# A two-layer hybrid block and a second block on one core: the first mixer rewritten as one interleaved program

## The reference, cut to what matters

```
z = rms_norm(h, norm_mix[0]) @ hy_w_in[0]
# delta rule: r, k, v, and three low-rank inputs (288 columns), each mixed with the token before
zr = zr + (token_shift(zr) - zr) * mu
w_log = -softplus(-(w0 + tanh(wd) @ w_up)) - 0.5; decay = exp(-exp(w_log))
a = sigmoid(a0 + ad @ a_up); g = sigmoid(gd) @ g_up
state = state * w_t - (state @ kk_t) (kk_t * a_t) + v_t k_t      # for each token
o = state @ r_t;  y_a = (group_norm(o) + sum(r * k * r_k) * v) * g
# state space
x_t = lam_bar * x_(t-1) + b_bar @ u_t ;  y = gelu(real(c_mat @ x_t) + d_skip * u)
y_b = y * sigmoid(y @ w_glu + b_glu)
h = h + concatenate([y_a, y_b]) @ hy_w_out[0]
```

## Time and profile before

| | us |
|---|---|
| three runs, median (lowest, highest) | 3212.8 (3207.9, 3220.8) |
| the profiled execution, its own time | 3210.8 |
| its span, first to last instruction | 3209.0 |
| PE busy in the span | 2824.6 |
| DVE busy | 2236.2 |
| ACT busy | 1650.6 |

### The profile page before, as it was taken

The page is one execution under the profiler, slowest core; times in us unless marked ns, Lnnn a source line. Parts: engine busy times, 40 slices in busy tenths (PEclk is TensorE's granted clock), DMA queues, the critical chain, the costliest instruction groups (busy, mean ns, idle before and its releaser), DMA issues.

```text
span 3209.0 us, 44097 instructions
## 1 busy us (share of the span) xinstructions
PE 2824.6 (88%) x18534; PEld 2523.0 (79%) x18534; DVE 2236.2 (70%) x2274; ACT 1650.6 (51%) x1569; POOL 0.2 (0%) x4
## 2 busy tenths in 40 slices
PE   6467017999997989999999999999999988998999
PEld 5357007999987978888888888888888778998899
DVE  2421784455565548888888888888888856886687
ACT  2200004444465536777776777777777645345443
POOL 0000000000000000000000000000000000000000
PEclk9776558999999989999999999999999989999999
DMA  5100003445542429999999999999999843554453
GB/s 194 40 2 1 0 0 121 142 145 184 171 130 68 158 110 342 357 353 346 354 356 346 348 352 352 353 353 350 352 354 358 324 138 119 184 171 132 132 184 132
DMA packets 237717, 690.50 MB, mean 215 GB/s; under 512 B 10448, under 2 KB 169168, under 8 KB 178128
## 3 DMA queue, kind: packets, MB, share of 16 engines
q1 hardware_dynamic: 235440, 685.59, 59.2%
q10 hardware_dynamic: 2080, 2.10, 0.2%
HBM read 686.59 MB, written 1.05 MB: 214 GB/s over the span
## 4 chain that ended last, share of the span: by engine, by line
PE 67%; DVE 7%; DMA 4%; ACT 3%; DVEq 2%; issue 1%; PEld 0%; PEldq 0%; ACTq 0%; SPq 0%
PE ps L716 20%; PE ps L718 20%; PE ps L717 20%; DMA ring<-moe 3%; PE ps L1462 1%; DVE more_lo L3095 1%; PE ps L776 1%; DVE w_lo L3095 1%; PE ps L1510 1%; DVE w_lo L1632 1%; ACT arena L1581 1%; PE ps L909 1%; ACT w_hi L1616 1%; DVE mix L2355 1%; PE ps L946 0%
## 5 line engine op out<-in xcount | busy, mean ns | idle before, releaser
L1632 DVE TENSOR_TENSOR w_lo<-ring,w_hi 128x1024 fp32r<-128x1024 f32 x362 | 437.5, 1222 | 372.1 <-ACT w_hi L1616 368.1
L1616 ACT ACTIVATE w_hi<-ring 128x1024 fp32r<-128x1024 f32 x362 | 380.3, 1057 | 465.0 <-PE ps L718 440.6
L716 PE MATMUL ps<-x_hi,w_hi 128*128 128x256 f32 x1952 | 563.3, 289 | 33.6 <-DVE x_lo L2349 17.6
L718 PE MATMUL ps<-x_hi,w_lo 128*128 128x256 f32 x1952 | 558.1, 286 | 0.0
L717 PE MATMUL ps<-x_lo,w_hi 128*128 128x256 f32 x1952 | 558.1, 286 | 0.0
L3095 DVE TENSOR_TENSOR w_lo<-ring,w_hi 128x2048 fp32r<-128x2048 f32 x232 | 522.7, 2284 | 15.3 <-ACT w_hi L1584 13.7
L1584 ACT ACTIVATE w_hi<-ring 128x2048 fp32r<-128x2048 f32 x232 | 445.3, 1920 | 159.9 <-DMA ring<-moe 133.3
L716 PEld LDWEIGHTS ps<-x_hi,w_hi 128*128 128x128 f32 x1952 | 380.5, 195 | 39.8 <-issue 38.5
L717 PEld LDWEIGHTS ps<-x_lo,w_hi 128*128 128x128 f32 x1952 | 380.6, 195 | 0.3
L718 PEld LDWEIGHTS ps<-x_hi,w_lo 128*128 128x128 f32 x1952 | 380.3, 195 | 0.0
L1584 ACT ACTIVATE more_hi<-ring 128x2048 fp32r<-128x2048 f32 x115 | 220.7, 1919 | 122.9 <-DMA ring<-moe 111.2
(11 more groups left out here) (339 smaller groups left out, 5068.4 us busy)
## 6 DMA issues: line engine op xcount, KB each, us to landing
ring<-moe SPq DMA_DIRECT2D x347, 1024.0 KB, 6.3
more_raw<-moe SPq DMA_DIRECT2D x115, 1024.0 KB, 6.5
ring<-ffn_w_up SPq DMA_DIRECT2D x44, 1024.0 KB, 5.1
ring<-ffn_w_down SPq DMA_DIRECT2D x22, 1024.0 KB, 4.8
ring<-xa_w_kv SPq DMA_DIRECT2D x16, 1024.0 KB, 5.5
ring<-w_in SPq DMA_DIRECT2D x16, 1024.0 KB, 5.8
ring<-da_w_qkv SPq DMA_DIRECT2D x12, 1024.0 KB, 5.1
ring<-ff_w_gate SPq DMA_DIRECT2D x11, 1024.0 KB, 5.3
```

Of the source, the lines that this page charges most:

```text
L716: mm(o, lhs[0], rhs[0], start=start, stop=False)
L718: return mm(o, lhs[1], rhs[0], start=False, stop=stop)
L1616: nc.scalar.activation(w_hi[:, half_slot(at, half), :], ring[:, s_, half * 1024:half * 1024 + 1024], ACT.Copy).then_inc(hi_ready, 1)
L1632: nc.vector.tensor_tensor(w_lo[:, i, :], ring[:, s_, half * 1024:half * 1024 + 1024], w_hi[:, i, :], ALU.subtract).then_inc(lo_ready, 1)
```

## The change

The three parts of the mixer become one program for each engine (`pe_first_mixer`, `act_first_mixer`, `dve_first_mixer`), in which the work of the projections, the delta rule and the state-space half is interleaved by hand, and each hand-over has a semaphore of its own; the meetings of all engines are gone from the mixer.

- Load order: h, a narrow head of the small inputs and of the constants, the 288 columns, the two chunks for u, then the remaining small inputs and constants, then k, r, v.
- State-space half: eight half rounds of two state tiles; the table of waves is built in four parts of four state tiles, each when it is needed (`s5_table`). The real and imaginary products are no longer added on DVE: four products go to PE, which adds them (`s5_sum`). It has PSUM banks 4 to 7, the delta rule 0 to 3; its buffers lie over x_hi, x_lo, act_hi and act_lo.
- Delta rule: products and their copies take turns in its four banks. In the recurrence both halves alternate (`halves`), the product of kappa and v is made ahead for all chunks, and the state of each chunk has a buffer of its own, so the next state needs only beta·u; the output of a chunk is multiplied after its change of state. The first chunk has no product with the state, which is zero.
- Output projection: the rows of `hy_w_out` are exchanged, so the state-space half comes first; the first two of its four chunks are multiplied in halves around the group norm (`out_half`), inside the mixer. `pe_memory` starts with the sums of the memory norm and chunks 2 and 3.

The diff, cut to its core:

```diff
+            sp.dma_start(h[:, :, :], x_t.rearrange("(k p) n -> p k n", p=P)).then_inc(h_loaded, 16)
+            sp.dma_start(small_sb[:, 0:HEAD_W], small[:, 0:HEAD_W]).then_inc(head_loaded, 16)
+            sp.dma_start(const_sb[:, 0:CONST_HEAD_W], const[:, 0:CONST_HEAD_W]).then_inc(head_loaded, 16)
             hy = w["hy_w_in"][0]
-            stream_columns(sp, at, hy, 0, 3 * RW)
             stream(sp, at, hy[:, 3 * RW:3 * RW + 288], 288)
             stream_columns(sp, at, hy, 3 * RW + 288, 4 * RW + 288)
+            sp.dma_start(small_sb[:, HEAD_W:SMALL_W], small[:, HEAD_W:SMALL_W]).then_inc(small_loaded, 16)
+            sp.dma_start(const_sb[:, CONST_HEAD_W:CONST_W], const[:, CONST_HEAD_W:CONST_W]).then_inc(const_loaded, 16)
+            for c in (2, 3, 0, 1, 4, 5):
+                stream_columns(sp, at, hy, c * CH, (c + 1) * CH)
...
+        def halves():
+
             for t in range(RT):
-                cs, ts = slice(t * P, (t + 1) * P), slice(t * S, (t + 1) * S)
-                mm(banks(0, 2)[:, ts], sm("lora")[0:64, cs], zg[0:64, 0, :], start=True, stop=True)
-                mm(banks(2, 2)[:, ts], sm("lora")[64:128, cs], zg[64:128, 0, :], start=True, stop=True)
-            for t in range(RT):
-                cs, ts = slice(t * P, (t + 1) * P), slice(t * S, (t + 1) * S)
-                mm(banks(4, 2)[:, ts], sm("g_up")[:, cs], zg[:, 1, :], start=True, stop=False)
-                mm(banks(4, 2)[:, ts], sm("g_up2")[0:32, cs], zg[0:32, 2, :], start=False, stop=True)
-                mm(banks(6, 2)[:, ts], cst("heads"), work[:, ts], start=True, stop=True)
-            pe.drain().then_inc(met, 1)
-            pe.wait_ge(met, at.step("lora products, sums for kk"))
-            pe.drain().then_inc(met, 1)
-            pe.wait_ge(met, at.step("sigmoids"))
-            pe.drain().then_inc(met, 1)
-            pe.wait_ge(met, at.step("cumulated decays, root for kk"))
-            pe.drain().then_inc(met, 1)
-            pe.wait_ge(met, at.step("exponentials, kk"))
-            pe.drain().then_inc(met, 1)
-            pe.wait_ge(met, at.step("alpha, beta, kappa, rho"))
+                yield t, HALF[0]
+                yield (t + 2) % RT, HALF[1]
+
+        def by_tile(hs, pair, t, off=0):
+            return ps[hs, 2 * pair + t // 2, off + (t % 2) * C:off + (t % 2) * C + C]
...
+            def level(i):
+                pe.wait_ge(below_ready, i + 1)
+                if i:
+                    pe.wait_ge(level_added, i)
+                for j, hs in problems():
+                    last = mm(pbank(0)[hs, j, :], below[i % 2][hs, j, :], tri[hs, j, :], start=True, stop=True)
+                last.then_inc(across_done, 1)
+                pe.wait_ge(across_out, i + 1)
+                for j, hs in problems():
+                    mm(pbank(2)[hs, j, :], tri_t[hs, j, :], xbuf[hs, j, :], start=True, stop=True)
+                for j, hs in problems():
+                    last = mm(pbank(0)[hs, j, :], xbuf[hs, j, :], tri_t[hs, j, :], start=True, stop=True)
+                last.then_inc(level_done, 1)
+
+            def state_by_alpha(c):
+                pe.wait_ge(chunk_state, c)
+                for t, hs in halves():
+                    last = mm(by_tile(hs, c % 2, t), tat[hs, 4 * t + c, :], state[c][hs, t, :], start=True, stop=True)
+                last.then_inc(u_done, 1)
+
+            def state_change(c):
+                if c:
+                    pe.wait_ge(chunk_u, c)
+                    pe.wait_ge(o_out, c)
+                for t, hs in halves():
+                    last = mm(by_tile(hs, 1 - c % 2, t), beta_tok[hs, 4 * t + c, :], u_chunk[c][hs, t, :],
+                              start=True, stop=True)
+                last.then_inc(change_done, 1)
...
+            def chunk_output(c):
+                if c == 3:
+                    pe.wait_ge(chunk_u, c)
+                for t, hs in halves():
+                    j = 4 * t + c
+                    o = by_tile(hs, c % 2, t, P)
+                    if c:
+                        mm(o, state[c][hs, t, :], ar[hs, j, C:2 * C], start=True, stop=False)
+                    mm(o, u_chunk[c][hs, t, :], neg_nt[hs, j, :], start=c == 0, stop=False)
+                    last = mm(o, v_tok[hs, j, :], w_t[hs, j, :], start=False, stop=True)
+                last.then_inc(o_done, 1)
...
+            pe.wait_ge(head_loaded, 32)
+            pe_norm(pe, at)
+            lora_inputs()
+            chunk(1, x_ready(pe, at))
+            chunk(2)
+            pe.wait_ge(small_loaded, 16)
+            pe.wait_ge(const_loaded, 16)
+            lora_products()
+            chunk(3)
+            gate_product()
+            s5_drive(0)
+            chunk(4)
+            chunk(5)
+            kk_sums()
+            chunk(6)
+            pe.wait_ge(kk_terms, 2)
+            s5_sum(0)
+            chunk(7)
+            s5_drive(1)
+            chunk(8)
...
+            pe.wait_ge(turned_out, 6)
+            pe.wait_ge(masked_out, 5)
+            level(0)
+            s5_sum(2)
+            level(1)
+            s5_sum(3)
+            s5_drive(4)
+            level(2)
...
+            s5_drive(7)
+            pe.wait_ge(level_added, 5)
...
+            pe.wait_ge(solved_out, 3)
+            pe.wait_ge(solved_out, 4)
+            state_change(0)
+            chunk_output(0)
+            s5_sum(7)
+            state_by_alpha(1)
+            state_change(1)
+            chunk_output(1)
+            state_by_alpha(2)
+            state_change(2)
+            chunk_output(2)
+            state_by_alpha(3)
+            chunk_output(3)
+            pe.wait_ge(s5_activated, 1)
...
+            pe.wait_ge(s5_gate, 1)
+            out_half(pe, at, 0, 0, x, 4, mixed)
+            by_heads(0, 2, gn_sq, var_done, gn_squared)
+            by_heads(1, 3, gn_sq, var_done, gn_squared)
+            out_half(pe, at, 1, 0, x, 5)
+            out_half(pe, at, 0, 1, x, 4, mixed)
+            out_half(pe, at, 1, 1, x, 5)
...
+            act.wait_ge(lora_mixed, 1)
             activate(zg[0:64, 0, :], zg[0:64, 0, :], ACT.Tanh)
             activate(zg[:, 1, :], zg[:, 1, :], ACT.Sigmoid)
-            activate(zg[0:32, 2, :], zg[0:32, 2, :], ACT.Sigmoid)
-            act.drain().then_inc(met, 1)
-            act.wait_ge(met, at.step("lora inputs, squares of kk"))
-            act.drain().then_inc(met, 1)
-            act.wait_ge(met, at.step("lora products, sums for kk"))
+            activate(zg[0:32, 2, :], zg[0:32, 2, :], ACT.Sigmoid).then_inc(lora_ready, 1)
+            split_hi_half(act, at, 0)
+            evac(out(u_t[:, 0:2, :], 1))
+            split_hi_half(act, at, 1)
...
+            def s5_table(g):
+                gs = slice(4 * g, 4 * g + 4)
...
+                    shape = [P, 4, m]
+                    lo, hi = slice(0, m), slice(m, 2 * m)
+                    t = s5b(2 * g, 0)[:, :, :].rearrange("p (a b) n -> p (a b n)", b=2).rearrange(
+                        "p (j n) -> p j n", n=P)[:, :, 0:m]
+                    products(e_re[:, :, hi], e_re[:, :, lo], scalars(pr, shape), e_im[:, :, lo], scalars(pi, shape), SUB, t)
+                    products(e_im[:, :, hi], e_re[:, :, lo], scalars(pi, shape), e_im[:, :, lo], scalars(pr, shape), ADD, t)
...
+            def s5_in(i):
+
+                er, ei = (e[:, 2 * (i % 2):2 * (i % 2) + 2, :] for e in (e_re, e_im))
+                vr, vi = ps[:, 4:6, 0:S], ps[:, 4:6, S:2 * S]
+                zr, zi, t = s5b(i, 0), s5b(i, 1), s5b(i, 2)
+                if i > 1:
+                    dve.drain()
+                dve.wait_ge(s5_driven, i + 1)
+                products(zr, er, vr, ei, vi, ADD, t)
+                nc.vector.tensor_tensor(zi, er, vi, MUL)
+                nc.vector.tensor_tensor(t, ei, vr, MUL).then_inc(s5_turned, 1)
+                dve.drain()
+                tt(dve, zi, zi, t, SUB)
+
+            def s5_scan(i):
+                for q in range(2):
+                    n = 2 * i + q
+                    a = mag[:, n:n + 1].to_broadcast([P, S])
+                    nc.vector.tensor_tensor_scan(s5b(i, 2)[:, q, :], a, s5b(i, 0)[:, q, :], 0.0, MUL, ADD)
+                    nc.vector.tensor_tensor_scan(s5b(i, 3)[:, q, :], a, s5b(i, 1)[:, q, :], 0.0, MUL, ADD)
+                dve.drain()
+
+            def s5_out(i):
+
+                er, ei = (e[:, 2 * (i % 2):2 * (i % 2) + 2, :] for e in (e_re, e_im))
+                yr, yi = s5b(i, 2), s5b(i, 3)
+                if i:
+                    dve.wait_ge(s5_summed, i)
+                nc.vector.tensor_tensor(s5b(i, 4), er, yr, MUL)
+                nc.vector.scalar_tensor_tensor(s5b(i, 5), ei, -1.0, yi, MUL, MUL)
+                nc.vector.tensor_tensor(s5b(i, 6), er, yi, MUL)
+                nc.vector.tensor_tensor(s5b(i, 7), ei, yr, MUL).then_inc(s5_ready, 1)
...
+            def next_state(c):
+
+                before = by_chunk[:, :, c, :]
+                if c:
+                    tt(dve, passed, state[c], before, ADD)
+                    before = passed
```

(38 more changed lines are left out.)

1020 lines of the change are left out of this document (530 added, 490 removed).

## The result

The changed kernel takes 3039.25 us (median of 4 runs, 3034.3 to 3042.35) where the kernel before took 3214.25 beside it (4 runs): ratio 0.944, 95% interval 0.9422 to 0.9458. The profiled execution is 3034.3 us with a span of 3032.5. The forecast was 3063, which is 29 us above the profiled run and 24 above the median: the direction and what bounds the mixer were right, the size of three terms was not.

A forecast was written before the change was run, and what follows sets the result against it. DVE's queue, the longest of three, bounds the interleaved mixer: 311 us through waits and hand-offs, then 21, 39 and 15 give 386 against 534.2, 148 less, so 3063 us; own range 3045 to 3085, over all cases 3035 to 3108.

The forecast's parts named there:

- second rival: Whole kernel: DVE's cost is less than summed and the high clock holds, 3035 us (3020 to 3045); chance 10%.
- A, the start: From kernel start to the split of the third projection chunk, with h loaded first: 44 us.
- B, DVE's queue: DVE's summed operations from the third chunk's split to the last state-space output, four tables included: 247 us.
- C, the waits and hand-overs: DVE's waits for PE or ACT inside its queue, 15 us, plus 5 us for some 30 late hand-offs.
- PE needs about 10 us for a level: Delta rule's five levels: PE passes of 3.7, 3.6 and 2.0 plus ACT's copy 1.2; DVE waits 3, 0, 0, 2, 0.
- the 18 us of PE behind the last level: After the last delta-rule level: PE's four products with three copies, 18 us against DVE's 14, so DVE waits 4.
- The 5 us for hand-overs: Some 30 late hand-offs at 0.17 us each, the idle before DVE's first product after a barrier.
- D, the recurrence: Four chunks of the recurrence at 5.3, 5.5, 5.5 and 4.6 us, an alternated pass at 0.057: 21 us.
- E, to the second output chunk: From the recurrence through glu product and group norm to the end of the first two output chunks: 39 us.
- F: Sums of the memory norm and two more output-projection chunks, 112 passes: 15 us.
- PE as the bound: Mixer: PE at half clock, its single queue delaying chunks, levels and sums; adds 30 to 50, 3103 us; chance 20%.
- the side where DVE's idle stays: From 102 to 534 us: removed barriers only marked true dependences; 3262 us with no idle gone; chance 3%.

The follow-up runs named there:

- one table: Changed kernel without the second, third and fourth table of waves (wrong waves used): last output 61.8 us earlier, 62.5 us in the medians.
- shared powers: Changed kernel with wave powers and first four doubling levels made once for all 16 state tiles: 35.3 us earlier at the recurrence, 35.4 in the medians.
- more waits: Changed kernel with 309 already satisfied semaphore waits before DVE's products: 0.3 us at the recurrence, 0.0 in the medians.
- halves apart: Changed kernel with the recurrence's 16 passes of one half of the rows before the other's, not alternating: 20.35 us instead of 14.26 to the last output.
- one after the other: Changed kernel with half rounds 1 to 7 and their three tables put behind the delta rule's recurrence: 70.9 us slower in the medians, 0.968 of the kernel before.

## Why the prediction was off by 24 to 29 us

The median, 3039.25, lies below the forecast's own range (3045 to 3085) and in that of its second rival (3020 to 3045). By terms, the forecast's arithmetic gives:

- **The bound: right.** DVE's queue from 41 to 290 us sets the mixer (one table, shared powers: 68 and 35 us taken from DVE, 62 and 35 us gained). At its end the bound is shared: behind the last addition, at 276 us, PE's products with ACT's copies and the first change of state end at 290.3, and DVE's two half rounds at 290.4, so less work for DVE there alone should gain nothing (not tested).
- **A, the start:** 44 forecast, 41.3 measured. ACT's first square begins at 9.73 us (7 + 1.3 + 0.3 = 8.6 in the forecast), and the steps behind it are shorter (the norm 13.9 instead of 15.1).
- **B, DVE's queue:** 247 forecast, 245 measured (41.3 to 290.4 us less 4.1 of idle). The tables' extra 50 us were real: four at 22.8 against 43.5 before.
- **C, the waits and hand-overs: wrong.** 15 + 5 forecast, 4.1 measured, of which one real wait. The step that failed first is "PE needs about 10 us for a level": it needed 7.1, 8.4 and 7.1 in the three levels with short covers (the first, third and fourth), and the 3 + 2 us of waits didn't come. With levels made long (12 to 13.5 us), waits of 10.5 us appear where the covers are short. The second is the 18 us of PE behind the last level, forecast against DVE's 14 with a wait of 4: PE and ACT took 13.3 (276.14 to 289.46), although two of the four products still ran at the low speed. The V products made DVE wait 2 instead of 4, the hiccups were the 2 forecast. The 5 us for hand-overs were wrong by themselves (more waits).
- **D, the recurrence: wrong.** 21 forecast, 12.3 measured (290.4 to 302.7). I took 0.057 us for an alternated pass from a row at half the clock, though the row two below it had 2.03 us for 64 passes. At the full clock the recurrence's passes took 0.029. The structure, alternation (6.1 us, with the clock's part in it) and order (3.7 us, the same), was rightly named.
- **E, to the second output chunk:** 39 forecast, 33.2 measured (302.7 to 335.9): the gate product took 7.17 instead of 9.85 us and the state-space halves of x were ready 12.2 us behind the recurrence instead of 16; the first half chunk took 4.4 us where the forecast's times leave 5.5, and it did run in part at half speed, as I had assumed (0.21 us from pass to pass from 316 us on, 0.12 before); the rest is 0.9 in the steps behind it. **F:** 15 forecast, 15.1 measured.
- **The rest:** nothing forecast, +7 us in this profile. DMA bounds its middle part in both kernels, and a load of experts takes 6.9 us to land in the median against 6.3; the profiles of the other kernels have a stretch 3 us shorter to 17 us longer behind the memory sums. By the medians, with the mixer's end taken from each profile, this rest is 0 to 9 us longer than before in all fifteen kernels (an estimate), so the change may have a small part in it; what it would be stays open.

Sum: -2.7 (A), -2 (B), -16 (C), -8.7 (D), -5.8 (E), +7 (rest) = -28, the 29 us between 3063 and 3034. One cause, PE at half its clock in my prices, stands behind C's waits before the levels, nearly all of D and part of E. I had bounded it at 3 us in C, 3 in D and 4 in E; C's real waits came out 11 lower, D 9, E 6. A recount by passes would have shown D's at least: the recurrence has 272, and at half the price they are 8 us less, not 3. (The expectation for halves apart says 288; the 16 too many don't change its verdict.) The granted clock of 0.67 for the whole stretch was no ground for pricing every pass at half level: the earlier trace rows had both speeds in one level, 3.68 and 2.03, and the new order's mean is only 0.77. The rival whose time came nearest, 3035, was right about the clock in the two levels where the forecast had waits and in the recurrence, and wrong that DVE's operations cost less than summed. PE as the bound (3103) and the side where DVE's idle stays (3262) didn't occur.

Undone one at a time, the parts of the change cost: interleaving 74 us, load order 10, alternation 6, order in the recurrence 4, output beside the norm 3, together 97, if they add, of the 183 us before the last output pass; the tables cost 48. What is left, 134 us, is the removed meetings, the delta rule's first part beside the projections and the faster passes: not undone one by one, and how it divides among them is not shown. One reading of it: from one level's start to the next took 13.7 us between barriers (215.17 to 228.89 before) and 10.3 with its own semaphores (179.13 to 189.43). But of these 3.4 us the faster passes are 2.5, as the timeline of PE before shows: its level takes 9.7 us from the first pass to the last one's end, where the new one takes 7.1.

```profile
215.17 3.11 PE L1016 MATMUL ps<-arena 64*64 64x64 f32 x64 [4.03 <-ACTq L1912]
219.44 3.55 PE L1022 MATMUL ps<-arena 64*64 64x64 f32 x64 [1.16 <-ACTq L1917]
222.82 2.03 PE L1024 MATMUL ps<-arena 64*64 64x64 f32 x64
```

The idle before a level's first pass, 4.03 us here, is 2.55 in one after the other, where no other work stands between: some 1.5 us a level for own semaphores and a mask made ahead.

## What to carry to other kernels

When a queue of small dependent operations is the bound, sum that queue and trust the sum: it was right within 1% over 250 us, and 62 of 68 us and 35 of 35 taken off it came back. Price the engines beside it at both levels of the clock, each from its own row, and carry both sums to the end: a mean clock over a stretch doesn't say which passes run at which level. Work moved to another engine is not off the queue when it holds the queue's operations meanwhile. Tables built piecewise are cheap to store and dear to build: what depends on no piece (here powers and first levels) is built once.

## What the hardware showed that I had not expected

- 309 satisfied waits in front of DVE's operations, many of them 0.16 us short, cost 0.3 us in all.
- An idle of 16 us in front of PE (8 passes in it) costs its next work 1.9 us, while pauses of 4.4 us inside each level keep parts of it at half speed: 3.68 us for 64 passes that otherwise take 2.08.
- POOL needs 2.00 us for a masked product of 1024 elements, 1.8 times DVE's 1.13, and holds DVE's products and scans from SBUF for that time: moving 5.6 us of work to it cost DVE 7.4.
- Alternating the halves of the rows brings 16 passes of 64 columns from 0.96 to 0.68 us at the full clock.
